# One fused streaming-encoder layer on one core: search pieces, score placement, folded reciprocals and the order of the post-norm

## The reference, cut to what matters

```python
h = rmsnorm(x, g_pre); proj = h @ w_in                       # 2048 prompt rows, 32 sample rows
u_a, gate_a, q, k, v, qi, ki, wi, gate_b = split(proj)
y_a = pool_mixer(u_a)                                        # trailing windows 2/4/8/16, per-group linear
score = sum_h(wi * relu(qi @ ki.T)) * INDEX_SCALE            # 8 index heads
score = where(key_chunk <= query_chunk, score, -inf)         # chunks of 64
sel = top_k(score, 256)                                      # per query
p = softmax(q @ k[sel].T * 64**-0.5 + rel_bias[bucket])      # 8 heads, 2 key heads
out = concat(y_a * silu(gate_a), (p @ v[sel]) * silu(gate_b)) @ w_out
y = x + rmsnorm(out, g_post)                                 # the post-norm
```

## Time and profile before

| what | value |
|---|---|
| median of 3 executions | 1710.84 us (1708.82 to 1711.71) |
| the profiled execution | 1709.82 us |
| its span, first to last instruction | 1708.0 us |
| mean granted TensorE clock | 0.966 |
| PE busy | 1571.0 us, 92% of the span |
| DVE busy | 1212.5 us, 71% |
| ACT busy | 893.6 us, 52% |
| POOL busy | 473.1 us, 28% |
| DMA | 120.76 MB, 70 GB/s over the span |

### The profile page before, as it was taken

How to read it: one execution, slowest core, us unless ns; L and a number is a source line. 1 busy time by engine, 2 the same in 40 slices (tenths; PEclk the granted TensorE clock), 3 DMA queues, 4 the chain that set the end, 5 groups by cost and what they waited for, 6 DMA issues and landing times.

```text
span 1708.0 us, 17799 instructions
## 1 busy us (share of the span) xinstructions
PE 1571.0 (92%) x5191; PEld 877.6 (51%) x5191; DVE 1212.5 (71%) x2940; ACT 893.6 (52%) x1684; POOL 473.1 (28%) x384
## 2 busy tenths in 40 slices
PE   7999899989998989887888988999999999899996
PEld 4555555555555867655444444444444444455552
DVE  5412555557767878875549999999998999985422
ACT  3112333344434334452299988998888786523331
POOL 0112111121112112111344443433433333322241
PEclk9999999989999989988899999999999999999999
DMA  9312322221111110047533222220230211201001
GB/s 360 73 39 49 95 52 53 63 70 60 51 52 49 41 59 32 35 149 199 163 93 102 63 67 56 82 84 25 60 87 25 51 33 30 62 11 39 31 32 49
DMA packets 91978, 120.76 MB, mean 71 GB/s; under 512 B 17149, under 2 KB 63805, under 8 KB 91498
## 3 DMA queue, kind: packets, MB, share of 16 engines
q1 hardware_dynamic: 90506, 115.44, 21.7%
q10 hardware_dynamic: 1376, 4.19, 2.1%
HBM read 76.06 MB, written 43.54 MB: 70 GB/s over the span
## 4 chain that ended last, share of the span: by engine, by line
PE 23%; DVE 17%; ACT 6%; issue 5%; POOL 2%; POOLq 0%; DVEq 0%; ACTq 0%
PE wide L1648 7%; PE wide L1633 7%; DVE above L345 6%; DVE max_junk L1711 3%; ACT act_junk L1542 2%; PE bank L1613 2%; PE bank L1614 2%; PE bank L1615 2%; PE bank L1618 2%; POOL E L1501 1%; PE bank L1599 1%; DVE den L1727 1%; ACT E L1576 1%; DVE reach L383 1%; DVE S L379 1%
## 5 line engine op out<-in xcount | busy, mean ns | idle before, releaser
L931 PE MATMUL bank<-hT,home 128*128 128x512 f32 (+2 forms) x1280 | 489.5, 523 | 4.6 <-ACT kq L831 2.0
L1501 POOL TENSOR_TENSOR E<-E,home 128x512 f32<-128x512 f32 (+1 forms) x174 | 251.9, 1451 | 446.6 <-ACT E L1576 446.5
L931 PEld LDWEIGHTS bank<-hT,home 128*128 128x128 f32 x1280 | 241.2, 195 | 173.3 <-issue 150.6
L1633 PE MATMUL wide<-E,home 128*128 128x512 f32 x544 | 284.8, 605 | 9.9 <-POOL E L1501 9.7
L1576 ACT ACTIVATE E<-bank 128x512 f32<-128x512 f32 (+1 forms) x290 | 165.5, 571 | 244.9 <-PE bank L1618 243.2
L907 ACT ACTIVATE relu<-wide 128x1024 f32<-128x1024 f32 (+7 forms) x192 | 153.3, 802 | 173.5 <-PE wide L949 98.9
L1183 DVE SCALAR_TENSOR_TENSOR S<-relu,wi,S 128x1024 f32<-128x1024 f32 (+7 forms) x168 | 175.1, 1042 | 78.6 <-ACT relu L907 68.9
L1711 DVE CUSTOM_DVE_ANT_0 max_junk<-bank,mask 128x512 bf16<-128x512 f32 (+3 forms) x230 | 136.9, 614 | 68.9 <-PE bank L1599 55.4
L1648 PE MATMUL wide<-home 128*128 128x512 f32 x272 | 142.3, 614 | 23.2 <-ACT osb L1568 23.0
L949 PE MATMUL wide<-kiT,qiT 96*128 96x512 f32 (+3 forms) x304 | 136.4, 520 | 23.5 <-ACT relu L907 23.4
L1542 ACT ACTIVATE act_junk<-S,minus_cand 128x1152 bf16<-128x1152 f32 (+5 forms) x105 | 155.4, 1480 | 1.4
(11 more groups left out here) (204 smaller groups left out, 2390.0 us busy)
## 6 DMA issues: line engine op xcount, KB each, us to landing
xs<-x_prompt SPq DMA_DIRECT2D x16, 512.0 KB, 4.1
home<-w_in SPq DMA_DIRECT2D x16, 512.0 KB, 13.2
xr<-x_prompt SPq DMA_DIRECT2D x16, 512.0 KB, 4.3
y_prompt<-osb SPq DMA_DIRECT2D x16, 512.0 KB, 2.9
first_q<-q_high_scratch SPq DMA_DIRECT2D x24, 256.0 KB, 5.1
s_scratch<-S SPq DMA_DIRECT2D x11, 512.0 KB, 2.7
first_q<-q_low_scratch SPq DMA_DIRECT2D x18, 256.0 KB, 4.1
gb<-gb_scratch SPq DMA_DIRECT2D x17, 256.0 KB, 5.4
```

Source lines behind the costliest of these rows:

```text
L931: mm = pe.matmul(out, stationary(c), moving(c), start=(c == 0), stop=(c == DC - 1))
L1501: pool.tensor_tensor(E[:, k % 4, :, 0:n], E[:, k % 4, :, 0:n], EB[:, kv * GRP:(kv + 1) * GRP, off:off + n], ALU.mult)\
L1633: pe.matmul(wide[0][:, kv * 512:kv * 512 + GRP * n].rearrange("p (j n) -> p j n", j=GRP), values[:, kt, kv:kv + 2, :].rearrange("p a d -> ...
```

## The change

In the projection part, search pieces have four rounds instead of two, and scores are laid into all projections from block 2 on. With that the last search ends at the end of block 2 instead of in block 4. In the attention part:

- The post-norm of steps 6 to 15 stands at 0.80, behind the maxima and the shift, and GpSimd's residual at the end of its list.
- The reciprocal of tiles 5 to 14 (`FOLDED`) is folded: SP copies one row of sums per key head as 64 rows of 8, DVE inverts 8 columns at 0.4 of the step, SP writes them to DRAM and reads them back, spread over 64 partitions; GpSimd's mean waits for that, at two thirds of its list.
- The shift is one product with broadcast operands instead of eight.
- ACT only copies the output halves out of the bank (at 0.46 and 0.96); one square over both halves (`Z`) reads the copy at 0.06 of the next step. TensorE waits for one ACT instruction per half, and the post-norm has one sum instead of two to add.

```diff
-SEARCH_PIECES = [(r, r + 2) for r in range(0, ALL_ROUNDS, 2)]
+SEARCH_PIECES = [(r, min(r + 4, ALL_ROUNDS)) for r in range(0, ALL_ROUNDS, 4)]
...
-            taking = [last or step[0] == "Q" for step in mine]
+            taking = [b >= 2 or step[0] == "Q" for step in mine]
...
+        r_dram = dram("reciprocal_scratch", (2, NKV, 1, GRP * P))
...
+    FOLDED = range(FIRST - 1, NPT - 1)
...
+    def long(t):
+        return FIRST <= t < ST
...
     def dve_step(t):
...
-                        ([("I", t - 1)] if 0 <= t - 1 < NT else [], 0.2, 0.2),
-                        ([("P", t - 3)] if 0 <= t - 3 < NT else [], 0.5, 0.5),
                         ([("S", t + 1)] if 0 <= t + 1 < NT else [], 0.79, 0.79),
+                        ([("I", t - 1)] if 0 <= t - 1 < NT else [], *((0.4, 0.4) if t - 1 in FOLDED else (0.2, 0.2))),
+                        ([("P", t - 3)] if 0 <= t - 3 < NT else [], *((0.80, 0.80) if long(t) else (0.5, 0.5))),
                         ([("C", u)] if searched(u) else [], 0.9, 0.9))
...
     def act_step(t):
...
-                        ([("Y", t - 2, 0)] if 0 <= t - 2 < NT else [], 0.5, 0.5),
-                        ([("Y", t - 2, 1)] if 0 <= t - 2 < NT else [], 1.0, 1.0))
+                        ([("Y", t - 2, 0)] if 0 <= t - 2 < NT else [], 0.46, 0.46),
+                        ([("Y", t - 2, 1)] if 0 <= t - 2 < NT else [], 0.96, 0.96),
+                        ([("Z", t - 3)] if 0 <= t - 3 < NT else [], 0.06, 0.06))
...
+                def fold(t):
+
+                    i, turn = t % 2, t - FOLDED[0]
+                    sp.wait_ge(sums_out, 4 * (t + 1))
+                    for kv in range(NKV):
+                        sp.dma_start(folded[kv * HD:(kv + 1) * HD, i],
+                                     den[kv * HD:kv * HD + 1, i].rearrange("p (a n) -> p a n", a=HD))\
+                          .then_inc(folded_in[i], 16)
+                    sp.wait_ge(recip_done, t + 1)
+                    sp.dma_start(r_dram[i].rearrange("k o (a n) -> (k o a) n", a=HD), folded[:, i]).then_inc(folded_out, 16)
+                    sp.wait_ge(folded_out, 16 * (turn + 1))
+                    for kv in range(NKV):
+                        sp.dma_start(den[kv * HD:(kv + 1) * HD, i], r_dram[i, kv].broadcast_to([HD, GRP * P]))\
+                          .then_inc(spread_in, 16)
...
                         load_S(t + 4)
+                    if t - 1 in FOLDED:
+                        fold(t - 1)
                     if t >= 3:
...
                 def mean(t):
 
-                    pool.wait_ge(recip_done, t + 1)
+                    if t in FOLDED:
+                        pool.wait_ge(spread_in, 32 * (t - FOLDED[0] + 1))
+                    else:
+                        pool.wait_ge(recip_done, t + 1)
...
-                        if i == len(todo) // 3 and 0 <= t - 1 < NT:
+                        if i == (2 if t - 1 in FOLDED else 1) * len(todo) // 3 and 0 <= t - 1 < NT:
                             mean(t - 1)
-                        if i == 2 * len(todo) // 3:
-                            if t - 3 >= 0:
-                                residual(t - 3)
+                        if i == (len(todo) if long(t) else 2 * len(todo) // 3) and t - 3 >= 0:
+                            residual(t - 3)
...
                             act.wait_ge(o_full, 2 * b + i + 1)
-                            if 2 * b + i:
-                                act.wait_ge(o_free, 4 * b + 2 * i)
-                            act.activation(sq[:], wide[1][:, 0:512], ACT.Square,
-                                           accum_out=ss2[:, b, i:i + 1]).then_inc(o_free, 1)
                             if i == 0 and b >= 2:
                                 act.wait_ge(y_out[b % 2], 16 * (b // 2))
                             act.activation(osb[:, b % 2, i * 512:(i + 1) * 512], wide[1][:, 0:512], ACT.Copy).then_inc(o_free, 1)
+                        elif kind == "Z":
+                            b = at[0]
+                            act.wait_ge(o_free, 2 * b + 2)
+                            act.activation(sq[:], osb[:, b % 2], ACT.Square, accum_out=ss2[:, b:b + 1])\
+                               .then_inc(squared, 1)
...
-                    if c == 0 and 4 * t + 2 * i:
-                        pe.wait_ge(o_free, 4 * t + 2 * i)
+                    if c == 0 and 2 * t + i:
+                        pe.wait_ge(o_free, 2 * t + i)
...
-                    for h in range(NH):
-                        ins = dve.tensor_scalar(shift[:, t % 2, h, :], identb[:], nmax[:, h:h + 1], None, ALU.mult)
-                    ins.then_inc(shift_done, 1)
+                    dve.tensor_tensor(shift[:, t % 2], identb[:].rearrange("p (a n) -> p a n", a=1).broadcast_to([P, NH, P]),
+                                      nmax[:].rearrange("p (h n) -> p h n", n=1).broadcast_to([P, NH, P]), ALU.mult)\
+                       .then_inc(shift_done, 1)
...
                 def invert_sums(t):
+                    if t in FOLDED:
+                        dve.wait_ge(folded_in[t % 2], 32 * (1 + (t - FOLDED[0]) // 2))
+                        dve.reciprocal(folded[:, t % 2], folded[:, t % 2]).then_inc(recip_done, 1)
+                        return
...
                 def post_norm(t):
                     nonlocal n
-                    dve.wait_ge(o_free, 4 * (t + 1))
-                    link(dve.tensor_tensor(root[:, 3:4], ss2[:, t, 0:1], ss2[:, t, 1:2], ALU.add))
-                    dve.wait_ge(dk, n)
-                    n = inverse_root(dve, dk, n, root[:, 0:1], root[:, 1:2], root[:, 2:3], root[:, 3:4], 1.0 / D)
+                    dve.wait_ge(squared, t + 1)
+                    n = inverse_root(dve, dk, n, root[:, 0:1], root[:, 1:2], root[:, 2:3], ss2[:, t:t + 1], 1.0 / D)
```

More of the change, by code:

```diff
@@ L278, in build @@
         phase1(nc, A, sb, sem, identf, identb, onesb, k2, home, loaded, unit, xs, first_q, banks, wide, q_dram, gb_dram,
-               ma_dram, s_dram, m_dram, g_dram, k_dram)
+               ma_dram, s_dram, m_dram, g_dram, k_dram, r_dram)
         phase2(nc, A, sb, sem, identf, identb, onesb, k2, home, loaded, unit, xs, first_q, banks, wide, q_dram, gb_dram,
-               ma_dram, s_dram, m_dram, g_dram, k_dram)
+               ma_dram, s_dram, m_dram, g_dram, k_dram, r_dram)
 def inverse_root(dve, done, n, ms, y, tmp, ss, scale):
@@ L409, in phase1 @@
 def phase1(nc, A, sb, sem, identf, identb, onesb, k2, home, loaded, unit, xs, first_q, banks, wide, q_dram, gb_dram, ma_dram,
-           s_dram, m_dram, g_dram, k_dram):
+           s_dram, m_dram, g_dram, k_dram, r_dram):
     steps, inside = phase1_steps()
@@ L1313, in phase2 @@
         mask = sb(st, "mask", [P, 3, SEQ], BF16)
+        sq = sb(st, "sq", [P, D], BF16)
         act_junk = sb(st, "act_junk", [P, SEQ], BF16)
@@ L1328, in phase2 @@
         yT = sb(st, "yT", [P, 2, 4, P], F32)
-        sq = sb(st, "sq", [P, 512], BF16)
+        folded = sb(st, "folded", [P, 2, NH], F32)
         mxp = sb(st, "mxp", [P, NH, 4], F32)
         nmax = sb(st, "nmax", [P, NH], F32)
-        ss2 = sb(st, "ss2", [P, NT, 2], F32)
+        ss2 = sb(st, "ss2", [P, NT], F32)
         root = sb(st, "root", [P, 4], F32)
@@ L1361, in phase2 @@
         sums_out, recip_done = sem("sums_out"), sem("recip_done")
+        folded_in = [sem(f"folded_in{i}") for i in range(2)]
+        folded_out, spread_in = sem("folded_out"), sem("spread_in")
         mean_done, yT_done = sem("mean_done"), sem("yT_done")
-        o_full, o_free = sem("o_full"), sem("o_free")
+        o_full, o_free, squared = sem("o_full"), sem("o_free"), sem("squared")
         post_done = sem("post_done")
@@ L1526, in _ @@
                 waiting = []
-                for t in range(NT + 2):
+                for t in range(NT + 3):
                     for kind, *at in act_step(t):
```

## The result

The changed kernel takes 1689.9 us (median of 4; 1688.7 to 1690.8) where the kernel before, on the same chip, takes 1711.3 (1708.8 to 1714.0): ratio 0.988, 95% interval 0.986 to 0.989. The forecast was 1661 in 1630 to 1690. The direction was right and the time is at the very end of the range; the gain is 21 us where I forecast 50. The profiled execution took 1689.3 us, its span is 1687.5, its granted clock 0.963.

A forecast was written before the change was run, and what follows sets the result against it. DVE was taken to bound attention steps 6 to 13, and to hold up TensorE in projection blocks 3 and 4. 1709.8 - 20 (projection) - 30 (attention) = 1659.8, or 1661 as a median; range 1630 to 1690 us.

The forecast's parts named there:

- -20: Projection half: sum of its terms in us, from four-round search pieces that end all searches in block 2.
- -27: Blocks 3 and 4: 73 us of DVE work moved out, TensorE sets the pace; -27 us, bounds -10 and -34.
- Rival A: Only the attention part pays, as block 2 turns DVE-bound in its four-round pieces: 1679 us, chance 0.15.
- 8 x 0.344 = 2.75 us: Attention steps: DVE time of the old eight-instruction shift; one 1.22 us product replaces it, -1.5 us a step.
- my -30: Attention half: sum of its terms in us, -24 of it from DVE relief.
- The residual, two products' length, takes the gap before the next near keys. Nothing: GpSimd's list: residual moved from 2/3 to the end costs nothing (0 to +4 us with the mean's move).
- +1.3 (0 to +2.6): Attention steps: DVE's waits for GpSimd with the post-norm among the bias products, us a step.
- 3.0 x 8 = -24: Attention steps 6 to 13: 3.0 us a step cashed of 3.5 net DVE relief; bounds -12 and -37 us.
- The cover: Behind the last maximum: DVE's some 20 us of work against TensorE's 15 us and three banked maxima; costs 1 to 2 us.
- B: Only the projection part pays; DVE relief meets ACT and GpSimd at once, 1.5 us a step: 1675 us, chance 0.15.
- C: Slower: fold late, GpSimd waits in the mean and bias products hold TensorE; 1721 us at a 20 us trip, chance 0.04.
- the 14 us: Post-norm: by the port rule alone, one GpSimd block per small instruction, up to 11 x 1.28 = 14 us more.

The follow-up runs named there:

- fastest one: Kernel with post-norm and residual in the middle and the mean late, changed so that GpSimd does the residual ahead of the mean: 1655.9 us, 0.969.
- middle order: Changed kernel with post-norm back at 0.5 and residual back at 2/3 of GpSimd's list, mean still late: 1671.1 us, 0.977.
- old order: Changed kernel with every moved piece of DVE and GpSimd back where it was, only the new instructions kept: 1660.9 us, 0.970.
- extra product: Kernel with post-norm and residual in the middle, plus a product of the residual's size at the end of GpSimd's list: 1687.1 us, 0.986.

## Why the prediction was right in the projection part and wrong in the moves

**Projection part: right, by its own mechanism, term sizes off.** I took -20; it is -31 (median) or -30 (first shift). Blocks 3 and 4 gave 31 against -27 (-34 was my bound), block 1 the +1 that I took, block 2 +1 instead of +6. Pieces of four rounds did not turn block 2 DVE-bound; DVE's 170 us of work, as I summed it, were 163 of 187. Rival A falls.

**DVE relief: right for the reciprocal and the new shift, too large for the old shift.** The folded reciprocal takes 0.193 us (0.2 taken), the new shift 1.23 (1.22 taken). But the old shift was never 8 x 0.344 = 2.75 us: the durations of short instructions overlap. One step of the kernel before, in DVE's timeline:

```profile
1193.19 1.70 DVE L1721 TENSOR_SCALAR shift<-identb,nmax 128x128 bf16<-128x128 bf16 x8
```

From its start to the next instruction's start the old shift took 1.6 to 2.5 us in steps 5 to 14, 2.2 in the mean, the new one in the changed kernel 1.1 to 2.2, 1.3 in the mean. So the term was 0.9 us a step, not 1.5, and the medians give the shift 1 to 4 us in all.

**What failed: the price of the late post-norm and residual, and what a DVE microsecond buys.** The time is 29 us above the forecast. The projection part gave 11 us more than I took and the new instructions 11 less (-19 for -30), which cancel; the moved pieces cost 29, where my -30 had held only 1.3 a step for them. The late post-norm and residual account for all of the 29 by themselves: 28.9 with the old instructions, 30.8 with the new ones.
- "The residual, two products' length, takes the gap before the next near keys. Nothing". GpSimd's list had that gap. DVE's choice of keys lies in the same gap, and the two collide: 14.5 us by taking the residual back, 16.0 by putting a like product there alone, both with the post-norm in the middle.
- "+1.3 (0 to +2.6)" a step of port waits for the post-norm. Its own instructions in steps 7 to 13 of the changed kernel take 12.4 us more than in the fastest one, 1.8 a step, inside the range. With the choice and the rest it is 19.1 / 7 = 2.7 a step, just outside. But I added them to the time one for one: these 19.1 us of DVE stand beside 36.3 us of longer steps.
- "3.0 x 8 = -24". Relief on DVE was not cashed at that rate even where nothing had moved: the fold takes 3.15 us off DVE in each of ten steps and gave 6.
- The mean moved from a third to two thirds, "Nothing". In the changed kernel that held (1691.7 without the move, 1689.9 with it). In the middle order it costs 10.2 us, since the move trades places with a wait: GpSimd used to stand still through the post-norm, at the residual. All of it came back when the residual went ahead of the mean.

"The cover ... costs 1 to 2 us of the 4.6, counted" held up better than I thought at first sight of the trace, as far as these runs can tell. From the `nmax` of one step to the next step's first maximum, DVE's stretch takes in steps 7 to 14 together:

| kernel | stretch, steps 7-14 | length of steps 7-13 | DVE busy in them |
|---|---|---|---|
| projection part alone | 169.7 | 447.9 | 425.4 |
| fastest (residual ahead of the mean) | 163.6 | 433.3 | 401.9 |
| old order, new instructions | 165.5 | 436.8 | 403.9 |
| post-norm and residual in the middle | 164.9 | 449.4 | 413.4 |
| post-norm in the middle, residual late | 178.4 | 466.7 | 424.6 |
| changed | 209.4 | 469.6 | 421.0 |

The late residual adds 13.5 us to the stretch, 11.2 to DVE's busy time and 17.3 to the steps: that is collision. The late post-norm, on top of it, adds 31 to the stretch, takes 3.6 off DVE's busy time and adds 2.9 to the steps: most of what it puts behind the maxima it takes away from before them, and TensorE's waits for the maxima grow by 10 us. So the longer stretch isn't free, but beside a late residual it costs little in all. Where it shows is step 14: 79.3 us late, 75.7 in the middle. DVE time lost to collisions, 9 to 19 us in these steps between most pairs of orders, comes out as 1.3 to 1.9 times as much in the steps' length. One pair doesn't fit: from both pieces in the middle to the changed kernel DVE loses 7.6 us and the steps 20.2. That collisions make the loss is shown for the late residual and the late mean; how the rest divides between collisions, the longer stretch and the clock is not. (The first row's DVE time holds seven full reciprocals, which stood undisturbed in front of the last maximum.)

Together the three moves cost 1689.9 - 1660.9 = 29 us; without them the new instructions reach 1660.9, which is the forecast. That the numbers meet is luck: my -30 for the attention part is -19 (1680.1 to 1660.9), my -20 is -31.

**The terms in the old order.** From the medians: square -12.9, shift with it -0.6, fold -5.8, sum -19.3 against -30. I had cashed 3.0 of 3.5 us a step in eight steps. The sum is safe, the single terms less so: by the attention parts of the traces (the span less the first shift) they are -8.7, -7.8 and -2.4. In the fastest kernel the seven steps 7 to 13 became 14.6 us shorter, 2.1 a step, where DVE's time fell by 3.4 a step; TensorE is then busy for 94% of them. That its list is what limits them next is likely, not shown.

**Rivals.** B had the size (little cashed in the attention part) but not the cause: nothing met ACT. C's event is there, GpSimd waited 17.5 us in seven times for the spread (longest 4.1), but costs nothing that shows: with the mean back at a third these waits are 3.6 us and the time is 1691.7. I weighed the Trainium skill (SBUF — State Buffer, Who interferes with whom) against the stretched rows and took 1.3 us a step, since the 14 us that I had worked out from it were shown by nothing. The rows agree with its mechanism, an exclusive lock on a port pair that DVE and GpSimd share: two small instructions ended with the GpSimd product in which they began. The 14 us were my own working, one block for each small instruction, and don't come out: two of 11 were caught at the end of step 9, and 13 of 77 in steps 7 to 13. My 4 us for the fold's trip rested on what the Trainium skill (DMA: Bandwidth & Descriptors, Anatomy of one DMA) gives for a DMA that GpSimd issues; issued by SP here, the trip took 5.1. Of my own signs of being wrong, GpSimd waiting in the mean came true without being the cause, and "a post-norm of 6 us or more" nearly (5.0 to 5.5 us at the ends of steps 8 to 11); DVE's busy time over steps 7 to 13, to be 24 us less and in fact 4.4 less, was the sign to name.

**The clock.** The granted clock over steps 7 to 13 is 0.95 to 0.96 in the kernels where they take over 466 us, the changed one among them, and 0.98 to 1.00 where they take under 450. TensorE's busy time can't tell what that costs: 26 matmuls of these steps have no record in the traces of the projection part alone and of the fastest kernel. Of the 36.3 us that the changed kernel's steps are longer than the fastest one's, 22.8 are waits of TensorE (45.2 against 22.4 us); the other 13.5 are an upper estimate of what matmuls at a lower clock took (one with `identb` and the mask takes 403 ns in the mean instead of 392). Whether the clock would have stayed up without the waits, no run tells.

## What to carry to other kernels

Before you move work on one engine to where that engine has a gap, look at what the engines that share a path with it do in that gap: here two-input products on GpSimd and DVE's passes stretched one another, and two moves to "free" places cost 29 us. A wait that looks idle can be worth keeping: GpSimd standing at a semaphore was what kept a chain of eleven tiny instructions on DVE short. And relief on the busiest engine isn't cashed in full: 3 us a step off DVE gave 6 us in all, and freeing a bank one instruction earlier on ACT, at a slightly earlier place, gave 13.

## What the runs showed of the hardware

- A DVE instruction with one input is caught as well: the mask's write over 1280 columns, 0.49 us alone, took 2.31 beside a GpSimd product (in the kernel with the extra product).
- The stretch is mutual: GpSimd's residual took 2.38 us alone and 3.08 beside the choice.
- From the folded reciprocal through a write to DRAM and two spreads back to the product that needs them took 5.1 us.
- Durations of neighbouring short DVE instructions overlap: eight of 0.34 us in the mean took 1.70 in all.
